# Key selection by a bitwise threshold search on VectorE, and the causal convolution moved from GpSimd to VectorE, in a hybrid streaming encoder layer

## What is computed

```python
def dsa_attend(q, qi, wi, qcid, k_all, v_all, ki_all, kcid, n_sel):
    raw = jnp.einsum('bthi,bsi->bths', qi, ki_all)
    iscore = jnp.einsum('bth,bths->bts', wi, jax.nn.relu(raw))       # 4 indexer heads
    iscore = jnp.where(kcid[None, :] <= qcid[:, None], iscore, -jnp.inf)
    _, sel = lax.top_k(iscore, n_sel)     # 256 keys for the prompt, 36 for the samples
    ...                                   # softmax attention over the chosen keys
```

```python
def causal_conv(u, buf, w, b):
    up = jnp.concatenate([buf, u], axis=1)
    y = sum(up[:, j:j + T] * w[j] for j in range(CONV_W)) + b      # 512 channels, CONV_W = 4
    return y, up[:, -(CONV_W - 1):]
```

## Time and profile before

| | us |
|---|---|
| median of 3 runs | 1442.34 (1440.73 to 1445.07) |
| the profiled execution | 1444.74 |
| its span in the trace | 1442.0 |
| PE busy | 1230.0 (85%) |
| DVE busy | 823.2 (57%) |
| ACT busy | 448.3 (31%) |
| POOL busy | 407.8 (28%) |
| mean granted clock of PE | 0.886 of full |

### The profile page before, as it was taken

One profiled execution on the slowest core, in us unless ns is written; L12 is line 12 of the kernel. 1 busy time (PEld: TensorE's weight loads), 2 busy tenths in 40 slices (PEclk: granted clock), 3 DMA queues, 4 the chain that ended last, 5 costly groups with the idle time before them and its releaser, 6 DMA issues. The chain is left out here.

```text
span 1442.0 us, 18373 instructions
## 1 busy us (share of the span) xinstructions
PE 1230.0 (85%) x5971; PEld 680.2 (47%) x5972; DVE 823.2 (57%) x1947; ACT 448.3 (31%) x845; POOL 407.8 (28%) x469
## 2 busy tenths in 40 slices
PE   4899897999999368996767788999947999999990
PEld 3455454545554156674545567455534333333330
DVE  7148997699999456525999842232462322232237
ACT  6211113221111412103445453111214444444426
POOL 0011110105277422106827100644111222223310
PEclk9999898999999558655898899999957999999995
DMA  9300000001010200003000001444242779978446
GB/s 365 127 15 1 0 0 0 1 28 31 29 30 14 62 0 1 1 10 139 1 1 1 1 1 37 187 163 158 99 192 73 224 245 296 302 238 296 87 112 223
DMA packets 35770, 136.86 MB, mean 95 GB/s; under 512 B 9658, under 2 KB 12266, under 8 KB 30842
## 3 DMA queue, kind: packets, MB, share of 16 engines
q1 hardware_dynamic: 28218, 108.77, 20.3%
q0 software_dynamic: 7488, 27.27, 8.1%
HBM read 101.23 MB, written 34.80 MB: 94 GB/s over the span
## 5 line engine op out<-in xcount | busy, mean ns | idle before, releaser
L436 PE MATMUL p<-hT,p_wfm 128*128 128x512 f32 (+1 forms) x624 | 206.2, 493 | 2.1 <-PEq L106 2.1
L2160 PE MATMUL p_G<-p_wgu,p_xT 128*64 x416 | 185.0, 598 | 0.6 <-ACT p_xT L2085 0.6
L2162 PE MATMUL p_G<-p_high_gu,p_xT 128*64 128x512 f32 x416 | 184.9, 598 | 0.0
L450 PE MATMUL p<-p_wtm,hT 128*128 128x399 f32 (+1 forms) x480 | 171.1, 517 | 6.8 <-ACT p_relu L531 6.8
L436 PEld LDWEIGHTS p<-hT,p_wfm 128*128 128x128 f32 x624 | 105.3, 191 | 103.3 <-issue 103.3
L450 PEld LDWEIGHTS p<-p_wtm,hT 128*128 128x128 f32 (+1 forms) x480 | 88.3, 186 | 87.5 <-issue 18.4
L589 DVE MAX8 p_top<-p_score 128x8 f32<-128x272 f32 (+5 forms) x165 | 116.0, 703 | 12.1 <-DVE p_score L591 6.5
L2095 ACT COPY p_high_gu<-p_wgu 128x1024 f32 x104 | 101.0, 1042 | 39.1 <-issue 36.7
L591 DVE MATCH_REPLACE8 p_score<-p_top,p_score 128x272 f32<-128x272 f32 (+5 forms) x165 | 112.7, 683 | 0.0
L1981 POOL DMA_INDIRECT sum_rows<-p_ys,p_dest_of x26 | 55.2, 2122 | 198.2 <-DVE p_ys L2022 198.2
L2160 PEld LDWEIGHTS p_G<-p_wgu,p_xT 128*64 128x64 f32 x416 | 55.1, 137 | 110.0 <-issue 110.0
(11 more groups left out here) (431 smaller groups left out, 2147.8 us busy)
## 6 DMA issues: line engine op xcount, KB each, us to landing
p_wgu<-in_w_gu SPq DMA_DIRECT2D x16, 2048.0 KB, 9.2
p_wd<-in_w_down SPq DMA_DIRECT2D x16, 1024.0 KB, 12.3
p_wfm<-in_w_fm SPq DMA_DIRECT2D x13, 512.0 KB, 3.7
p_wtm<-in_w_tm SPq DMA_DIRECT2D x8, 598.5 KB, 16.2
p_x<-in_x SPq DMA_DIRECT2D x9, 512.0 KB, 9.3
h_rows<-p_x SPq DMA_DIRECT2D x9, 512.0 KB, 15.7
p_h<-h_rows SPq DMA_DIRECT2D x9, 512.0 KB, 3.4
h_rows<-p_h SPq DMA_DIRECT2D x9, 512.0 KB, 2.6
```

What stands on the lines that cost most here:

```text
L436: mm = nc.tensor.matmul(ps[3 * u + c][:, 0:b - a], w[:, u, k, :], m.hT[:, k, a:b], start=k == 0, stop=k == KD - 1)
L450: mm = nc.tensor.matmul(bank["tokens", n][0:rows, 0:TG], stream, m.wtm[:, k, g * TG:(g + 1) * TG], start=k == 0, stop=k == KD - 1)
L2160: nc.tensor.matmul(pG[u][low, :], xT[:, u, k, low], wgu[:, ds(slot, 1), k, :].rearrange("p a n -> p (a n)"), start=k == 0, stop=k == KD - 1)
L2162: mm = nc.tensor.matmul(pG[u][high, :], xT[:, u, k, high], high_gu[:, u, k, :], start=k == 0, stop=k == KD - 1)
```

## The change

- A prompt tile's 256th largest score (of tiles 1 to 7, `chosen`) is built bit by bit as an integer pattern. A pass counts, for each of the seven tiles, the scores that are at least as large as a trial value (`count`: compare, with the sum over the row as an accumulator output); there is one pass with 0.0 for the sign, then 31 with one bit set each. Three small instructions on 128x7 values stand around each pass.
- `first_ties` counts the scores above the threshold in one more pass, and then, for each tile, marks the scores equal to it, takes their prefix sum with a scan, keeps the first `need` of them, and writes `m.bias`.
- All nine tiles' scores are made first, with nothing between them on DVE. PE's `order` stays as it is. Tile 7's rounds in the attention phase are gone. The sample tile keeps its 5 rounds, behind the bit search.
- The convolution is on DVE, behind all of that, with a fused multiply-add (SCALAR_TENSOR_TENSOR) in place of the two instructions.
- The constants get 31 more columns.

```diff
@@ -65,7 +65,7 @@
-                  ("iota16", NE), ("unit_rows", TOK // UNIT), ("rowid", TT), ("slotid", UNITS), ("bfm", FM)):
+                  ("iota16", NE), ("bits", 31), ("unit_rows", TOK // UNIT), ("rowid", TT), ("slotid", UNITS), ("bfm", FM)):
@@ -257,7 +257,6 @@
-LEFT = [NT - 1] * (TOPK_P // 8)
@@ -314,10 +313,14 @@
-        acc, part = both("acc", [P, ALL]), both("part", [P, PROMPT // 2 + P])
+        acc = both("acc", [P, ALL])
-        bfm, top = cols(m, "bfm"), al("top", [P, 8])
+        late_spare = al("late_spare", [P, NK[1]])
+        bfm, top, one = cols(m, "bfm"), al("top", [P, 8]), al("one", [P, 1])
+        chosen = [t for t in range(NT) if NK[t] > TOPK_P]
+        cnt, need = al("cnt", [P, len(chosen)]), al("need", [P, len(chosen)])
+        best, trial, step = (al(n, [P, len(chosen)], I32) for n in ("best", "trial", "step"))
@@ -390,35 +393,7 @@
-                pool.wait_ge(conv_in, 32)
-                pool.wait_ge(relu_used, n_relu)
-                own = Chain(pool, pool_own)
                 g = nc.gpsimd
-                for c in range(4):
-                    pool.wait_ge(fm_copied, 3 * (F_BQ + c) + 3)
...
-                    for j in range(1, 4):
-                        for x, y in ((j, half), (half, PROMPT)):
-                            own.link(g.tensor_scalar(part[:, 0:y - x], u[:, x - j:y - j], tap(3 - j), None, ALU.mult))
-                            own.link(g.tensor_tensor(acc[:, x:y], acc[:, x:y], part[:, 0:y - x], ALU.add))
-                        own.link(g.tensor_scalar(parts, up[:, :, 3 - j:SLEN + 3 - j], tap(3 - j), None, ALU.mult))
-                        ins = g.tensor_tensor(accs, accs, parts, ALU.add)
-                        if j < 3:
-                            own.link(ins)
-                    ins.then_inc(acc_ready, 1)
 
@@ -575,42 +550,81 @@
-                def top_keys(t):
-                    N, n = NK[t], (TOPK_P if t < NT else TOPK_S + EXTRA) // 8
-                    n -= LEFT.count(t)
-                    if n == 0:
-                        return
-                    if N <= TOPK_P and t < NT:
-                        key_bias(nc, own, m, t, None)
...
+                def count(limit, i, t, op=ALU.is_ge):
+                    at = KEY_AT[t]
+                    return nc.vector.tensor_scalar(m.bias[:, at:at + NK[t]], score_of(m, score, t, 0, NK[t]), limit, 0.0, op, ALU.add,
+                                                   accum_out=cnt[:, i:i + 1])
+
+                def bit_search():
+                    for i, t in enumerate(chosen):
+                        ins = count(0.0, i, t)
+                    own.link(ins)
+                    own.link(nc.vector.tensor_scalar(best[:, :], cnt[:, :], float(TOPK_P), -1.0, ALU.is_lt, ALU.mult))
+                    for b in range(31):
+                        bit = cols(m, "bits")[:, b:b + 1].bitcast(I32)
+                        own.link(nc.vector.tensor_tensor(trial[:, :], best[:, :], over(bit, [P, len(chosen)]), ALU.bitwise_xor))
+                        for i, t in enumerate(chosen):
+                            ins = count(trial[:, i:i + 1].bitcast(F32), i, t)
+                        own.link(ins)
+                        own.link(nc.vector.tensor_scalar(step[:, :], cnt[:, :], float(TOPK_P), float(1 << (30 - b)), ALU.is_ge, ALU.mult))
+                        own.link(nc.vector.tensor_tensor(best[:, :], best[:, :], step[:, :], ALU.bitwise_xor))
+
+                def place_of(t):
+                    return late_spare[:, 0:NK[t]] if t == 1 else score[:, 0:NK[t]]
+
+                def first_ties():
+                    limit = lambda i: best[:, i:i + 1].bitcast(F32)
+                    for i, t in enumerate(chosen):
+                        ins = count(limit(i), i, t, ALU.is_gt)
+                    own.link(ins)
+                    own.link(nc.vector.tensor_scalar(need[:, :], cnt[:, :], -1.0, float(TOPK_P), ALU.mult, ALU.add))
+                    for i, t in enumerate(chosen):
+                        at, N = KEY_AT[t], NK[t]
+                        tie, x, tmp = m.bias[:, at:at + N], score_of(m, score, t, 0, N), place_of(t)
+                        own.link(nc.vector.tensor_scalar(tie, x, limit(i), None, ALU.is_equal))
+                        own.link(nc.vector.tensor_tensor_scan(tmp, over(one[:, 0:1], [P, N]), tie, 0.0, ALU.mult, ALU.add))
+                        own.link(nc.vector.scalar_tensor_tensor(tmp, tmp, need[:, i:i + 1], tie, ALU.is_le, ALU.mult))
+                        own.link(nc.vector.scalar_tensor_tensor(tmp, x, limit(i), tmp, ALU.is_gt, ALU.add))
+                        own.link(nc.vector.tensor_scalar(tie, tmp, 0.0, NEG, ALU.is_equal, ALU.mult))
+                        own.link(nc.vector.memset(m.bias[0:64, at + N - 64:at + N], NEG))
+
+                def sample_keys():
+                    src = score_of(m, score, NT, 0, SK + EXTRA)
+                    for k in range((TOPK_S + EXTRA) // 8):
+                        own.link(nc.vector.max(top[:, :], src))
+                        own.link(nc.vector.match_replace(src, top[:, :], src, TAKEN))
+                    key_bias(nc, own, m, NT, src[:, 0:SK])
+
+                for t in range(TT):
                     scores(t)
-                    top_keys(t)
-                for t in range(4, TT):
-                    scores(t)
-                for t in range(4, TT):
-                    top_keys(t)
+                own.link(nc.vector.memset(one[:, :], 1.0))
+                key_bias(nc, own, m, 0, None)
+                bit_search()
+                sample_keys()
+                first_ties()
+
+                dve.wait_ge(conv_in, 32)
+                V = nc.vector
+                for c in range(4):
+                    dve.wait_ge(fm_copied, 3 * (F_BQ + c) + 3)
+                    if c:
...
+                    V.tensor_copy(last_p[:, c, :], u[:, PROMPT - 3:PROMPT])
+                    V.tensor_copy(last_s[:, c, :, :], us[:, :, SLEN - 3:SLEN])
+                    V.tensor_copy(up[:, :, 0:3], hist[:, c, :, :])
+                    own.link(V.tensor_copy(up[:, :, 3:SLEN + 3], us))
+                    V.tensor_scalar(acc[:, 0:PROMPT], u[:, 0:PROMPT], tap(3), tap(4), ALU.mult, ALU.add)
+                    own.link(V.tensor_scalar(accs, up[:, :, 3:SLEN + 3], tap(3), tap(4), ALU.mult, ALU.add))
+                    for j in range(1, 4):
+                        V.scalar_tensor_tensor(acc[:, j:PROMPT], u[:, 0:PROMPT - j], tap(3 - j), acc[:, j:PROMPT], ALU.mult, ALU.add)
+                        ins = V.scalar_tensor_tensor(accs, up[:, :, 3 - j:SLEN + 3 - j], tap(3 - j), accs, ALU.mult, ALU.add)
+                        if j < 3:
+                            own.link(ins)
+                    ins.then_inc(acc_ready, 1)
@@ -1328,22 +1342,9 @@
-                def late_rounds(done):
-                    nonlocal n_round
-                    while n_round < len(LEFT) and n_round * sum(weight) < len(LEFT) * done:
-                        late = LEFT[n_round]
-                        src = score_of(m, None, late, 0, NK[late])
-                        own.link(nc.vector.max(top[:, :], src))
-                        own.link(nc.vector.match_replace(src, top[:, :], src, TAKEN))
-                        n_round += 1
-                        if late not in LEFT[n_round:]:
-                            key_bias(nc, own, m, late, src)
-
...
-                    late_rounds(sum(weight[:p + 1]))
```

More of the change, by code:

```diff
@@ L391, in _ @@
                     nc.gpsimd.tensor_tensor(m.tm[0:rows, t, c], m.tm[0:rows, t, c], m.btm[0:rows, c], ALU.add).then_inc(bias_added, 1)
-                pool.wait_ge(conv_in, 32)
-                pool.wait_ge(relu_used, n_relu)
-                own = Chain(pool, pool_own)
                 g = nc.gpsimd
-                for c in range(4):
-                    pool.wait_ge(fm_copied, 3 * (F_BQ + c) + 3)
-                    if c:
-                        pool.wait_ge(silu_ready, c)
-                    u = m.fm[:, F_BQ + c, :]
-                    us = u[:, PROMPT:ALL].rearrange("p (i t) -> p i t", i=NSEQ)
-                    accs = acc[:, PROMPT:ALL].rearrange("p (i t) -> p i t", i=NSEQ)
-                    tap = lambda j: wc[:, c, j:j + 1]
-                    g.tensor_copy(last_p[:, c, :], u[:, PROMPT - 3:PROMPT])
-                    g.tensor_copy(last_s[:, c, :, :], us[:, :, SLEN - 3:SLEN])
-                    g.tensor_copy(up[:, :, 0:3], hist[:, c, :, :])
-                    own.link(g.tensor_copy(up[:, :, 3:SLEN + 3], us))
-                    g.tensor_scalar(acc[:, 0:PROMPT], u[:, 0:PROMPT], tap(3), tap(4), ALU.mult, ALU.add)
-                    own.link(g.tensor_scalar(accs, up[:, :, 3:SLEN + 3], tap(3), tap(4), ALU.mult, ALU.add))
-                    half = PROMPT // 2
-                    parts = part[:, half:half + P].rearrange("p (i t) -> p i t", i=NSEQ)
-                    for j in range(1, 4):
-                        for x, y in ((j, half), (half, PROMPT)):
```

(45 more changed lines are left out.)

4 lines of the change are left out of this document (1 added, 3 removed).

## The result

The changed kernel took 1497.88 us (median of 4 runs, 1497.09 to 1500.17) where the kernel before took 1441.53 us: 1.040 times as long, with a 95% interval of 1.036 to 1.044. It is slower by 56 us. The prediction said 1520 us, 1485 to 1560.

What follows compares the result with a forecast made beforehand. PE and DVE were taken to fill the projection phase, and DVE to bound attention until tile 6. Projection +100 us and attention -22 us gave +78 us, from a median of 1442.34 to 1520 us, range 1485 to 1560.

Steps and rivals of the forecast that it cites:

- Part 1: Projection phase, all scores first: PE's two stalls, 14.8 us, go, so DVE's last score ends at 258.3 us.
- Part 5: Convolution on DVE: block 0 at 519.3 us, PE held until then, three feature tiles behind; next phase 100 us later.
- Parts 2 to 4: DVE in the projection phase: a counting pass 5.85 us, the search 209.2, one more pass 6.1 and ties 33.1.
- rival B: Counting pass runs at 0.52 ns per element; at 3.5 us a pass, 78 us less, 1442 us; chance 0.08.
- Part 6: Attention phase without tile 7's 32 rounds: PE is the next bound, 22 us go (10 to 32).
- D: Projection phase: ACT's copies get past its wait, so PE is not held; 1495 us; chance 0.04.
- A: The forecast: counting pass at one element per 1.03 ns, PE held by ACT's wait; 1520 us; chance 0.82.
- E: Attention phase gives all of its 79 us and not 22; 1463 us; chance 0.02.

Runs made afterwards that it cites:

- e4_plain_compare: The changed kernel with every count replaced by a plain TENSOR_SCALAR without accumulator output, so it chooses other keys: 1422.5 us in one run.
- e5_copies_first: The changed kernel, convolution still on DVE, but ACT copies all feature tiles before it waits for the first convolution block: 1470.72 us.
- e1_conv_on_pool: The changed kernel with the convolution back on POOL as before; scores, bit search and ties stay: 1430.86 us.
- e6_last_tile_late: e1_conv_on_pool with tile 7's bit search taken out of the common passes and made in 35 steps beside the attention phase: 1431.36 us.

## Why the prediction came out as it did

The mechanism held in each step: DVE in one chain from the last score to block 0, ACT held in front of the convolution, PE idle until ACT's copy, three feature tiles behind it, and an attention phase that gives back a part. The total was 22 us too high (1520 against 1498). The two phases were 27 us too high together, by the sizes of their terms; the recurrent phase, put at nothing, took 2.2 us more, and the medians lie 56 us apart where the profiled spans lie 53. By the prediction's own parts, in us:

| part | forecast | measured |
|---|---|---|
| 1: last score ends | 258.3 | 250.9 |
| 2: a pass | 5.85 | 5.84 |
| 3: search | 209.2 | 206.8 |
| 4: pass and ties | 39.2 | 39.3 |
| 5: convolution block | 6.9 | 6.4 |
| 5: PE restarts | 522.5 | 510.9 |
| 5: three tiles with clock | 50.1 | 49.2 |
| 5: next phase | 586.8 | 572.9 |
| 6: attention phase | -22 | -35.4 |

**Part 1 was mis-sized by 7.4 us.** I gave back the two stalls, 14.8 us, and called the rest PE's own work in the same order. It was, but not at the same speed. Behind the second stall the kernel before shows

```profile
236.74 8.13 PE L450 MATMUL p<-p_wtm,hT 128*128 128x399 f32 x16
...
247.88 5.63 PE L450 MATMUL p<-p_wtm,hT 128*128 128x399 f32 x16
```

and the granted clock of that kernel in the stall, and behind it, was

```profile
224.20:232.10 7.90, 0.00 (x0) 0.00 (x0) 7.22 (x16) 0.43 (x1) 0.00 (x0) 0.75 0.00 0
232.16:245.00 12.84, 12.84 (x34) 7.54 (x38) 8.80 (x17) 5.56 (x13) 1.03 (x1) 0.62 0.00 0
```

The same 16 matmuls take 8.13 us right after the stall and 5.63 us later. Together with the scores at the second stall and the 112 matmuls behind the first (40.58 us, where the kernel before makes 112 in 37.81 elsewhere) the slower stretches come to some 8 us, which went with the stalls (22.1 us gained). I had looked for the clock behind the new gap, and not behind the old ones.

**Part 5.** The table load of 1.28 us is not in the path: it stands at 362.88 us, ahead of the wait, and I had put it behind. The block was 0.5 us and the tail (from the last SiLU to the next phase) 0.9 us shorter than I had put them. The rest of the 13.9 us came down the chain from parts 1 and 3. The clock behind the gap cost 2.1 us (49.2 against 47.1) where I said 3; the granted clock was still 0.50 up to 512 us and 0.89 up to 520.

**Parts 2 to 4 held.** The mask, the only row with an accumulator, was the right neighbour: 1.04 ns per element against 1.03. But the prediction had the mask at one length, which can't give a rate; its 1.03 was that of MAX8, and 0.52 ns with 0.27 us fixed would have fitted the mask's 0.45 us as well. Two other lengths of the mask in the trace of before would have carried it better: 301 ns for 144 elements and 636 ns for 464 are 1.05 ns per element. Here a rule that looked better for the change, the doubled rate of the plain instruction, would have given 1442 or less, and e4_plain_compare shows the price: rival B took 78 us off the forecast for a pass of 3.5 us, and measured were 75 us off the changed kernel's time for one of 3.42, so B was priced nearly rightly and the accumulator output is what decides between them.

**Part 6 was mis-sized by 13 us.** I divided PE's 108.47 us by its busy share of tile 7. But these 108.47 us were spent at a clock of 0.89, and without the rounds the clock was 1.00 and PE's time 93.4 us, which over 0.885 is 105.5; measured were 112.1. So both factors were off, in opposite directions: the clock by 17 us of the stretch, the busy share (0.83, not 0.885) by 7. The stretch ahead of tile 2, where I had 2.6 us from a single round, went from 32.3 to 26.5 us. The bound of -32 that I gave for a denser PE fell short of the -35.4.

**The rivals.** The time, 1498, lies near D's 1495, but D is not what happened: PE was held for 117 us, and e5_copies_first shows that without that hold it is 1471. D was 25 us below A in the prediction, and the projection phase of e5_copies_first is 22.1 us shorter than that of the kernel after: D's step was sized well, and stood on a sum that was 22 us too high. Reading the time alone would have picked the wrong case. E (the attention phase gives 79) is ruled out by the 35.4.

## What to carry to other kernels

Before moving work to an engine, list what is queued on its consumer behind the wait for it: here a convolution of four blocks of 6.4 us on DVE cost 67 us, because ACT's copies stood behind its wait and PE behind the copies. Extra work on DVE in the attention phase cost little while its total fitted the stretch (2.9 us for 31) and three quarters of its length beyond that (26.7 us for 35), so add up its busy time in the stretch first, and look for idle gaps of the length of a piece. And where a stall goes, price the slow clock behind it too.

## What the runs showed of the hardware

- The output form of one instruction decides its rate: TENSOR_SCALAR from f32 to bf16 over 1040 elements 779 ns, with an accumulator output 1292 ns.
- Beside GpSimd's work some of VectorE's instructions were stretched, and the counts were not. The `p_step` instruction of the search has a mean of 313 ns in e1_conv_on_pool, with the convolution on POOL, and of 171 ns in the kernel after, with POOL idle. In e5_copies_first a copy of three columns, 0.17 us elsewhere, took 3.20 us, beside a scaling of POOL whose mean is 3.18 us:

```profile
529.02 3.20 DVE L617 COPY p_last_p<-fm 128x3 f32<-128x3 f32 x1 [1.31 <-ACT fm L521]
```

  In e6_last_tile_late two instructions of 656 elements, 0.90 and 0.50 us in the kernel after, took 3.42 and 3.35 us in a row beside two such scalings, which themselves took 7.09 us and not 6.4:

```profile
456.69 3.42 DVE L619 SCALAR_TENSOR_TENSOR p_score<-p_score,p_best 128x656 f32<-128x656 f32 x1
460.15 3.35 DVE L620 TENSOR_SCALAR key_bias<-p_score 128x656 bf16<-128x656 f32 x1
```

  That these long ones coincide with the scalings is shown; no run took the scalings away.
- The second stall of PE in the kernel before was paid twice: 7.96 us of waiting, and some 5 us more in the work behind it, at a granted clock of 0.62. In the kernel after, with no stall there, the same rows are back at 5.63 us for 16 matmuls.
